# Two blocks of a language model on one core: the first memory's key projection is moved into the routing, in pieces

## The reference, cut to what matters

```python
def moe_swiglu(xn, router_w, w_gate_up, w_down):
    xf = xn.reshape(-1, d_)
    logits = (xf @ router_w).astype(jnp.float32)
    top_v, top_i = lax.top_k(logits, TOP_K)
    top_w = jax.nn.softmax(top_v, axis=-1)
    ...
    for e in range(N_EXPERTS):
        out = out + combine[:, e:e + 1] * swiglu(xf, w_gate_up[e], w_down[e])

def memory_read(q, mem_n, w_mem_kv):
    kv = mem_n @ w_mem_kv
    k, v = jnp.split(kv, 2, axis=-1)
    logits = jnp.einsum('bshd,bmhd->bhsm', q, k) * (d ** -0.5)
    ...

def hybrid_layer(x, mem, ...):
    proj = rmsnorm(x, pre_g) @ w_in
    ...
    y_mem = memory_read(mem_q, rmsnorm(mem, mem_norm_g), w_mem_kv) * jax.nn.silu(mem_g)
```

## Time and profile before

| | us |
|---|---|
| median of 3 runs (lowest, highest) | 2167.52 (2166.28, 2169.9) |
| the profiled execution, its own time | 2169.45 |
| its span in the trace | 2167.3 |
| TensorE busy | 2136.8 |
| VectorE busy | 1591.6 |
| ScalarE busy | 1332.4 |

### The profile page before, as it was taken

One profiled execution on the slowest core, in us unless ns is written; L12 is line 12 of the kernel. 1 busy time (PEld: TensorE's weight loads), 2 busy tenths in 40 slices (PEclk: granted clock), 3 DMA queues, 4 the chain that ended last, 5 costly groups with the idle time before them and its releaser, 6 DMA issues.

```text
span 2167.3 us, 27831 instructions
## 1 busy us (share of the span) xinstructions
PE 2136.8 (99%) x10935; PEld 1813.2 (84%) x10935; DVE 1591.6 (73%) x1339; ACT 1332.4 (61%) x1151; POOL 78.2 (4%) x67
## 2 busy tenths in 40 slices
PE   7999999999998999999999999999999999999998
PEld 5988888888787888888888888888888898898987
DVE  5577555466766888888888888888896667675665
ACT  4475534455656777777777777777665555456553
POOL 3100000000000000000000000000110000000000
PEclk9999999999998999999999999999999999999999
DMA  8554665555538999999999999999996534455442
GB/s 282 157 190 151 224 193 177 188 180 164 195 136 301 348 377 381 374 381 375 388 376 379 378 379 375 381 380 374 389 383 219 176 125 156 157 180 175 137 153 81
DMA packets 249166, 569.70 MB, mean 263 GB/s; under 512 B 12169, under 2 KB 14353, under 8 KB 248817
## 3 DMA queue, kind: packets, MB, share of 16 engines
q1 hardware_dynamic: 242368, 546.41, 70.5%
q0 software_dynamic: 5136, 16.70, 2.3%
q10 hardware_dynamic: 1568, 5.31, 0.6%
HBM read 562.60 MB, written 5.78 MB: 262 GB/s over the span
## 4 chain that ended last, share of the span: by engine, by line
PE 93%; DVE 3%; DMA 2%; ACT 1%; issue 0%; SPq 0%; DVEq 0%; ACTq 0%
PE bank L917 35%; PE bank L1178 9%; PE bank L1179 9%; PE bank L1182 9%; PE bank L923 9%; PE bank L1226 5%; PE bank L1219 5%; PE bank L1221 5%; PE bank L964 3%; DMA ring<-w_in 1%; DVE halves_r L2194 1%; DMA ring<-moe_w_down 1%; DVE w_low L2622 0%; PE bank L1321 0%; DMA ring<-w_out 0%; PE bank L990 0%
## 5 line engine op out<-in xcount | busy, mean ns | idle before, releaser
L2622 DVE TENSOR_TENSOR w_low<-ring,w_high 128x4096 fp32r<-128x4096 f32 x167 | 736.5, 4421 | 80.5 <-ACT w_high L1901 80.3
L1901 ACT ACTIVATE w_high<-ring 128x4096 fp32r<-128x4096 f32 x167 | 607.1, 3636 | 232.7 <-DMA ring<-moe_w_gate_up 137.9
L917 PE MATMUL bank<-halves_r,xT_high 128*128 128x512 f32 (+1 forms) x1856 | 562.3, 381 | 4.8 <-ACT halves_r L1671 3.2
L2194 DVE TENSOR_TENSOR halves_r<-ring,halves_r 128x2048 fp32r<-128x2048 f32 x175 | 391.2, 2264 | 155.1 <-ACT halves_r L1671 153.0
L917 PEld LDWEIGHTS bank<-halves_r,xT_high 128*128 128x128 f32 x1856 | 343.6, 189 | 71.7 <-issue 5.6
L1671 ACT ACTIVATE halves_r<-ring 128x2048 fp32r<-128x2048 f32 x175 | 326.4, 1892 | 111.8 <-DMA ring<-w_in 51.8
L1178 PE MATMUL bank<-w_high,xg_high 128*128 128x512 f32 x896 | 354.7, 396 | 1.7 <-DVE xg_low L2599 1.7
L1179 PE MATMUL bank<-w_high,xg_low 128*128 128x512 f32 x896 | 349.5, 390 | 0.0
L917 PE MATMUL bank<-halves_r,xT_low 128*128 128x512 f32 (+1 forms) x928 | 348.5, 380 | 0.0
L1182 PE MATMUL bank<-w_low,xg_high 128*128 128x512 f32 x896 | 221.6, 389 | 0.0
L917 PEld LDWEIGHTS bank<-halves_r,xT_low 128*128 128x128 f32 x928 | 175.3, 189 | 31.7
(11 more groups left out here) (392 smaller groups left out, 2312.8 us busy)
## 6 DMA issues: line engine op xcount, KB each, us to landing
ring<-moe_w_gate_up SPq DMA_DIRECT2D x224, 1024.0 KB, 10.6
ring<-moe_w_down SPq DMA_DIRECT2D x112, 1024.0 KB, 9.9
ring<-w_in SPq DMA_DIRECT2D x108, 1024.0 KB, 5.1
ring<-w_out SPq DMA_DIRECT2D x24, 1024.0 KB, 4.9
ring<-ffn_w_gate_up SPq DMA_DIRECT2D x22, 1024.0 KB, 5.2
ring<-ffn_w_down SPq DMA_DIRECT2D x11, 1024.0 KB, 4.9
ring<-w_mem_kv SPq DMA_DIRECT2D x8, 1024.0 KB, 5.2
ring<-w_branch_attn SPq DMA_DIRECT2D x4, 1024.0 KB, 5.1
```

The source lines that it names most:

```text
L917: return pe.matmul(o[:, a:a + n], x[:, c, b * P:(b + 1) * P], w[:, k, col:col + n], **flags)
L1901: act.activation(high_slot(k), ring[:, ring_r.slot(names[k]), :], ACT.Copy).then_inc(w_high_in[r], 1)
L2194: dve.tensor_tensor(raw_view(half, halves_r), raw_view(half), top_view(half).bitcast(F32), ALU.subtract).then_inc(raw_low_in, 1)
L2622: dve.tensor_tensor(w_low[:, slot, :], ring[:, slot, :], high_slot(k).bitcast(F32), ALU.subtract).then_inc(w_low_in[r], 1)
```

## The change

1. In the first block, `MK` of layer 0 joins the ring behind `WO`; SyncE issues its two halves ahead of the first expert's tiles, and `RAW_AT` and `TOP_AT` deal the halves otherwise. In the second block `MK` of layer 0 is gone. `MK` of layer 1 stays.
2. The 16 transposes of the memory move ahead of the transposes of block 0 of the tokens. ScalarE and VectorE form `mgk_high` and `mgk_low` (memory by gain, 8 chunks of 128x256 each) between the parts of the norm.
3. TensorE's 96 key products are cut in eight pieces (`memory_keys(k, h, top)`) and stand between the routing steps; the last 16 products stand between the gather and the first expert.
4. The three router products of a chunk become two: high by both parts of the router in one product of 16 columns, low by high in one of 8. VectorE adds the two parts.
5. The keys go over the DRAM: ScalarE copies them out of the banks behind the high part of expert 0's second tile and issues a transfer of 0.5 MB; GpSimd fetches them back in the second block.
6. VectorE makes the low part of expert 0's first tile in two halves around the parts of `xg_low`, and the weights of the routing later.
7. In the second block `MV` of layer 0 is made for both token blocks per half: high products of half 0, the scatter, low products, high products of half 1, the `P` transposes, low products.
8. TensorE's overflow body moves behind the second block. It is reached by a branch of its own and left by another; past it leads one jump at the program's end.

```diff
-RAW_AT, TOP_AT = (6, 7, 2, 3, 4), (5, 0, 1, 8)
+RAW_AT, TOP_AT = (2, 3, 4, 6, 7), (1, 5, 8, 0)
...
+    j += norm_jobs("E") if l == 1 else []
     j += norm_jobs("2", l, blocks=(0,)) + [("WO", l, 1, 1)]
...
-    "MK0 MK1 MV0 P00 P01 P10 P11 MV1 XB0 XB1 XB2 XB3 Z0 Z1 DT MQ0 MQ1 DN XT0 XT1 CB0 CB1 MG0 MG1 AC "
+    "MV0 MV1 P00 P01 P10 P11 XB0 XB1 XB2 XB3 Z0 Z1 DT MQ0 MQ1 DN XT0 XT1 CB0 CB1 MG0 MG1 AC "
...
-FIRST_HALVES = len(halves_of(first_tiles(0) + first_tiles(1)))
+FIRST_HALVES = len(halves_of(first_tiles(0) + first_tiles(1) + [("MK", 0)]))
...
                 by_block(("WO", l, 0), ("WO", l, 0), 1)
+                if l == 1:
+                    for b in range(TB):
+                        norm_turn(("E",), b, memS, (mem_x, b + 1))
                 norm_turn(("2", l), 0, xs, (norm_x, 4 * l + 3))
...
-                    pe.matmul(o[:, 8 * b:8 * b + 8], xT_high[:, c, s], router_high[:, c, :], start=first, stop=False)
-                    pe.matmul(o[:, 8 * b:8 * b + 8], xT_low[:, c, s], router_high[:, c, :], start=False, stop=False)
-                    mm = pe.matmul(o[:, 8 * b:8 * b + 8], xT_high[:, c, s], router_low[:, c, :], start=False, stop=last)
+                    pe.matmul(o[:, at_b:at_b + 2 * EXPERTS], xT_high[:, c, s], router_both[:, c, :], start=c == 0, stop=False)
+                    mm = pe.matmul(o[:, at_b:at_b + EXPERTS], xT_low[:, c, s], router_high[:, c, :], start=False,
+                                   stop=c == KC - 1)
...
+            def memory_keys(k, h, top):
+                half = (("MK", 0), h)
+                w = high_half(half) if top else low_half(half)
+                pe.wait_ge(mg_ready, 4 * h + 4)
+                if top and h == 0:
+                    keys[k] = begin(("EK", k))
+                cs = list(enumerate(half_chunks(*half)))
+                for j, a in ((2 * k, 0), (2 * k + 1, SEQ)):
+                    piece = cols(j, a)
+                    for q, c in cs:
+                        mm = piece(keys[k], mgk_high, w, c, q, start=top and h == 0 and q == 0 and a == 0,
+                                   stop=not top and h == 1 and q == len(cs) - 1 and a == SEQ)
+                        if top:
+                            mm = piece(keys[k], mgk_low, w, c, q, start=False, stop=False)
                 return mm
 
             logits = begin(("RT",))
             route_rows(logits, 0)
+            memory_keys(0, 0, True)
+            memory_keys(0, 0, False)
             norm_turn(("2", 1), 1, xs, (norm_x, 8))
+            memory_keys(1, 0, True).then_inc(top_free[tops.slot((("MK", 0), 0))], 1)
             pe.wait_ge(*drained(("X", "2", 1, 1, 1)))
             route_rows(logits, 1).then_inc(*end(("RT",)))
-            for b in range(TB):
-                norm_turn(("E",), b, memS, (mem_x, b + 1))
+            memory_keys(1, 0, False).then_inc(*raw_end((("MK", 0), 0)))
+            memory_keys(0, 1, True)
             pe.wait_ge(rt_mask, 1)
...
+            memory_keys(1, 1, True).then_inc(top_free[tops.slot((("MK", 0), 1))], 1)
+            def last_keys():
+                memory_keys(0, 1, False).then_inc(*end(("EK", 0)))
+                memory_keys(1, 1, False).then_inc(*end(("EK", 1)))
-            more = experts("m", sel_ready)
-            with pe.If(more > 0):
...
+            more = experts("m", sel_ready, last_keys)
+            pe.br_cond(more > 0, "tensor_overflow", "tensor_second_block")
...
+                if l == 0:
+                    weigh(("MV", l), [("MV0", [rows(0)]), ("MV1", [rows(1)])], l, x=mg, ready=mg_in,
+                          between={0: last_scatter, 1: norm_turns})
...
+            pe.br("tensor_done")
+            with nc.body("tensor_overflow", parent=home):
...
                 lower("2", l, 0)
...
+                    memory_low(range(KC // 2))
+                    link(dve.tensor_copy(lt_r, lt))
+                    link(dve.tensor_copy(ones_r, ones))
+                    residual_part(("WO", l, 1, 1), 1, 1)
+                    memory_low(range(KC // 2, KC))
+                    norm(1, 4 * l + 4, norm2_row)
...
                 if r == "m":
                     overflow()
-                    routing_weights()
+                    first_tile_low(0)
...
                 gathered(r, [("GX", r, 0), ("GX", r, 1)], 0)
                 if r == "m":
+                    first_tile_low(1)
+                    routing_weights()
```

More of the change, by code:

```diff
@@ L382, in kernel_program @@
             banks.lay(ffn_jobs(), kept=("FD",), silent=silent)
-    banks.lay([("RT",), *norm_jobs("2", 1, blocks=(1,)), *norm_jobs("E"), ("RK",)])
+    banks.lay([("RT",), *norm_jobs("2", 1, blocks=(1,)), ("EK", 0), ("EK", 1), ("RK",)], silent=silent)
     tiles.lay(expert_tiles("m"), EXPERTS, offsets=expert_slots())
@@ L569, in kernel_program @@
         xg_high = rounded("xg_high", [KC, P], xT_at)
+        early = Views(NHIGH * TILE)
+        mgk_high = rounded("mgk_high", [KC, SEQ], arena_at + 4 * early.at)
+        early(KC, SEQ)
+        memT_first = early(KC // 2, SEQ)
+        early = Views(NHIGH * TILE + TILE + P)
+        mgk_low = rounded("mgk_low", [KC, SEQ], arena_at + 4 * early.at)
+        early(KC, SEQ)
+        kmT_out = shaped(x_rows, 4, SEQ)
         rt = Views(ARENA - 256)(256)
@@ L946, in weigh @@
                         mm.then_inc(top_free[tops.slot(half)], 1)
-                    if between is not None and h == between[0]:
-                        between[1]()
+                    if between is not None and h in between:
+                        between[h]()
                     w = low_half(half)
@@ L1510, in _ @@
                 pe.wait_ge(*drained("YS1", l))
-                out_tile(2, between=(1, lambda: branch_turn("YR", yr, (ret_y, l + 1))))
+                out_tile(2, between={1: lambda: branch_turn("YR", yr, (ret_y, l + 1))})
                 last_out_tile()
+            pe.br("tensor_done")
+            with nc.body("tensor_overflow", parent=home):
+                pe.wait_ge(moe_done, 1)
+                for s in range(NSLOT):
+                    pe.sem_inc(f_tile_free[s], F_CREDIT)
+                for s in range(NBANK):
+                    pe.sem_inc(f_bank_free[s], F_CREDIT)
+                for n in range(2):
+                    pe.wait_ge(*drained(("Y", "m", n), EXPERTS - 1))
+                experts("f", f_sel_ready)
+                for n in range(2):
+                    pe.wait_ge(*drained(("Y", "f", n), EXPERTS - 1))
+                pe.wait_ge(f_done, 1)
+                pe.br("tensor_second_block")
+            nc.switch_bb("tensor_done", parent=home)
         @block.gpsimd
@@ L1825, in mixer @@
                     split(("FU", 0), (0,))
+                else:
+                    act.wait_ge(second_in, 16 * SECOND_LOADS)
+                    for job in norm_jobs("E"):
+                        act.wait_ge(*drained(job))
+                    for c in range(KC):
+                        src = memT_first if c < KC // 2 else memT[1]
+                        act.activation(mgk_high[:, c, :], src[:, c % 4, :], ACT.Copy,
+                                       scale=par_all[:, 0, 8 + c:9 + c]).then_inc(mem_copied, 1)
+                    split(("MK", 0), (1,))
                 norm(1, drained(("WO", l, 1, 1)))
@@ L1950, in experts @@
                     act.dma_start(hn_dram.ap().rearrange("(b p) d -> p b d", p=P), xs[:]).then_inc(hn_y_out, 16)
+                    for k in range(2):
+                        copy_out(kmT_out[:, 2 * k:2 * k + 2, :], ("EK", k), scale=HD ** -0.5)
+                    for k in range(2):
+                        act.wait_ge(*drained(("EK", k)))
+                    act.dma_start(km_dram.ap(), x_rows).then_inc(hn_y_out, 16)
+                    act.activation(memT[0], memT_first, ACT.Copy).then_inc(mem_copied, 1)
                     act.wait_ge(flag_ready, 1)
@@ L1958, in _ @@
             mixer(0)
[L1959 removed]
+            act.activation(router_high, router, ACT.Copy).then_inc(router_high_in, 1)
             ffn()
@@ L2487, in route @@
                 row8 = slots_row[:, 0:8]
[L2488 to L2495 removed]
                 dve.wait_ge(*full(("RT",)))
[L2497 removed]
+                both = out_of(("RT",))[:, 0:4 * EXPERTS].rearrange("p (b k e) -> p b k e", b=TB, k=2)
+                link(dve.tensor_copy(shaped(rt[:, 0:16], TB, 8), both[:, :, 0, :]))
+                link(dve.tensor_tensor(shaped(rt[:, 0:16], TB, 8), shaped(rt[:, 0:16], TB, 8), both[:, :, 1, :], ALU.add))
                 dve.sem_inc(*fr(("RT",)))
@@ L2678, in expert, with first_tile_low @@
                             output_low(r, e)
+                def first_tile_low(half):
+                    slot, a = tiles.slot(names[0]), half * HALF
+                    dve.wait_ge(w_high_in["m"], 1)
+                    ins = dve.tensor_tensor(w_low[:, slot, a:a + HALF], ring[:, slot, a:a + HALF],
+                                            high_slot(0)[:, a:a + HALF].bitcast(F32), ALU.subtract)
+                    if half:
```

(3 more changed lines are left out.)

148 lines of the change are left out of this document (79 added, 69 removed).

## The result

The changed kernel takes 2156.95 us (median of 4 runs, 2155.77 to 2158.86), the kernel before beside it 2167.53: ratio 0.9948, 95% interval 0.9936 to 0.9960, or 10.6 us less. The forecast was 2154.6, with a range of 2149 to 2161.5.

| stretch | before | after | difference |
|---|---|---|---|
| start to the end of `WO`'s second-last block | 652.00 | 653.03 | +1.03 |
| from there to expert 0 | 32.13 | 28.17 | -3.96 |
| expert 0 to the end of expert 7 | 952.62 | 953.86 | +1.24 |
| from there to `X0` | 30.58 | 19.52 | -11.06 |
| `X0` to the end | 499.97 | 502.52 | +2.55 |

A forecast was written before the change was run, and what follows sets the result against it. TensorE, busy 2136.8 of 2167.3 us, was taken as the bound. Routing 3.5 plus behind the experts 9.6 less experts' start 0.2 made 12.9 us: 2169.45 to 2156.5 profiled, median 1.9 below, 2154.6; range 2149 to 2161.5.

The forecast's parts named there:

- The bound: Whole kernel: TensorE, busy 2136.8 of 2167.3 us, bounds it; other engines count only where TensorE waits for them.
- The routing: `WO`'s second-last block to expert 0: products sum to 28.3 us, plus 0.3 of waits; 3.5 us gained, bounds none to 5.
- The covers: Routing: key products laid over TensorE's waits for other engines, each 0 to 1 us thicker than what it covers.
- The start of the experts: Expert 0's second tile: VectorE's low part done at 688.2, wanted at 689.7; 0.2 us lost, up to 1.5.
- Behind the experts: Expert 7 to `X0`: 19.8 us against 30.58, 10.8 gained, behind a new wait of 4.4; net 9.6, bounds 8 and 14.
- The clock at `X0`: Behind the new wait of 4.4 us at `X0`, the clock falls and costs 1.2 us (0 to 3).
- The queue: SyncE's weight transfers: the fourth expert tile lands at about 691, before 693.7 when wanted; cost nothing.
- 2 (the jump costs on): Behind expert 7: the jump isn't what costs 2.41, or the new branch costs as much; 3.9 less gained, 2158.5; chance 0.12.
- 3 (nothing from the routing): Routing: covers missed or clock stays down, expert 0 starts at 684 as before, 2158.1; chance 0.15.
- 4 (no wait at `X0`): At `X0`: new wait mostly not there and the clock holds; 4 more gained, 2150.6; chance 0.13.
- 5 (the clock falls behind 24 transposes): Routing's start at 652: clock falls behind 24 transposes in a row, costing 1.5, 2156.1; chance 0.06.
- 6 (fed late): Expert stage: weights come late and TensorE waits from the fourth tile on; 12.5 lost against 9.6 gained, 2170.4; chance 0.04.

The follow-up runs named there:

- experiment 4: Changed kernel without 80 of the 96 key products of the routing (work left out, keys wrong): 2160.08 us, ratio 0.9960 to the kernel before.
- experiment 6: Changed kernel with the router products apart again, 48 in all instead of 32: 2160.08 us, ratio 0.9963 to the kernel before.
- experiments 1 and 2: Kernel before with TensorE's overflow body moved behind the program's last product (1: 2162.61 us), or left in place but cut short (2: 2164.23 us).
- The second profile: Profile of the changed kernel run again without any edit: 2156.41 us, ratio 0.9941 to the kernel before.
- experiment 9: Changed kernel with the ring's halves dealt as before (`RAW_AT` and `TOP_AT` undone): 2174.62 us, ratio 1.0024 to the kernel before.
- experiment 8: Changed kernel with `xT`'s low parts ahead of `X0`'s low halves, and its high parts between `X0`'s high halves: 2149.62 us, ratio 0.9912.
- experiments 5 to 8: 5: changed kernel again, 2156.41 us; 7: changed kernel, last 16 key products ahead of the gather, 2157.76 us; 6 and 8 have their own lines.
- experiment 10: Experiment 8's kernel with TensorE's overflow body back between the experts and the second block: 2154.83 us, ratio 0.9932 to the kernel before.

## Why the prediction was right, step by step

**The bound.** TensorE, and stretches read by its busy share: right. The first stretch came out by the sum of its products. In the second TensorE is busy for 15.06 of 19.52 us and `X0` waits for VectorE, as the prediction had counted it.

**The routing, 3.5 forecast, 3.96 measured** (28.17 us against a sum of 28.3 and 0.3 of waits). The sum of products was right within 0.1 us, and the 0.3 of waits are not there. The covers are as thin as I had put them, 0.2 to 0.7 us. What the prediction undersold is why it pays: experiment 4 shows that the products in the holes gain by themselves, 3.3 us: without them five waits come back, and 17 us of half clock; and experiment 6 that the joined router products are part of that. The clock of the kernel before isn't a fixed loss: 32.13 in the profile that I read, 30.5 in two others. Of the 3.96, up to 1.6 was that draw. So what was forecast well is the stretch after; that the gain came out so near 3.5 is in part luck, and against the shorter 30.5 it would have been 2.3.

**The start of the experts, 0.2 forecast.** No wait there; the low part of the second tile ended 0.5 us before its use. The experts took 1.24 us more in the first profile and 0.56 in the second, within what they differ by anyhow.

**Behind the experts, 10.8 forecast ahead of the clock, 11.06 measured.** Part by part: counted from E, the end of expert 7, with the forecast in brackets: scatter at E+3.62 (3.65), VectorE's additions at E+4.28 (4.3), norm ended at E+12.5 (12.6), a wait at the transposes of 0.34 (0.6 and 0.35), `X0` at E+19.52 (19.8) behind 4.01 (4.4). The reading that the wait of 2.41 was the branch's and not VectorE's rested on the earlier trace rows; experiments 1 and 2 show that it is the skipped body's, and not VectorE's.

**The clock at `X0`, 1.2 forecast, 2.4 measured.** This is the term that was mis-sized. The price was taken from the fall of the earlier trace rows, 1.5 behind a gap of 2.41, and put lower; the wait of 4.0 brings the clock down in all seven profiles that have it, in three for 3.4 us and in four, the two of the changed kernel among them, for 6.8. Against the 500.2 from `X0` to the end without a fall it costs 1.4 or 2.4. So the two places gave 15.0 where the forecast had 14.3, and 2.5, 1.2 and 1.0 went off behind `X0`, in the experts and ahead of it all, where it had 1.2, 0.2 and nothing: 10.2 instead of 12.9. The second profile, with less of the chance, has 12.4.

**The queue, nothing.** Right under the new dealing. The fourth tile's transfer was issued at 681.4, with its weights there for ScalarE at 692.9 at the latest:

```profile
692.87 3.62 ACT L1970 ACTIVATE w_high<-ring 128x4096 fp32r<-128x4096 f32 x1
```

Its first product stood at 698.2, 1.7 behind the end of the high part. But the prediction passed over what the two tuples do; experiment 9 prices the question at 17 us.

**The rivals.** 2 (the jump costs on): refuted by 71 ns and no gap. 3 (nothing from the routing): refuted. 4 (no wait at `X0`): refuted in this kernel, and made true in experiment 8, where it gives 6.8 instead of my 4: the wait and, behind it, its clock. 5 (the clock falls behind 24 transposes): refuted, the clock stayed at 1.00 behind 653.03. By the Trainium skill, TensorE: Matmul & The Clock Gate, Part 4, a transpose doesn't count as busy in the same way; this trace shows no effect of it. What did come ahead of a fall without a gap was 24 router products in a row, in the one profile of experiment 6. 6 (fed late): refuted for this dealing; under the old one it is what happens, at expert 0 already.

Still open is how long the clock of the kernel before is down in an execution. Its nine executions beside experiments 5 to 8 suggest that this is a part of their spread: five with a mean clock of 0.996 had spans of 2164.9 to 2166.4 us, four with 0.994 or 0.995 had 2168.0 to 2169.1. Beside the other experiments the groups overlap (0.997 with 2168.2 us, 0.995 with 2165.8). The profile of experiment 10 has no fall at all and a mean clock of 1.000, as has one more of its executions (2150.7 us); the three with 0.999 took 2153.0 to 2153.6. A fall behind the gap in those three would explain why its median is further from that of experiment 8 than 2.3 us, but no trace shows it.

## What to carry to other kernels

Where a chain on other engines makes TensorE wait, fill the holes with products that are due anyway: here 96 products in the holes took less time than 16 of them, since waits and half clock came back without the others. Cut them by the length of the holes, and place them by what they cover, since the same 16 products ahead of the gather instead of behind it cost 1.9 us more. When work moves, look at what it used to cover: the keys had covered VectorE's work ahead of `X0`, and the exchange of two steps on VectorE and on ScalarE gave two thirds of the whole change once more. And ask of a buffer table which late reader holds the slot that the next stage wants first.

## What the runs showed of the hardware

- A conditional branch of TensorE over the whole overflow body took 6.1 to 6.7 us in three profiles and held products back by 2.2 to 2.8; over some 20 instructions it took 210 ns, and into the code that follows 71 ns. The table of waits put the gap down to VectorE each time.
- Behind a gap of 2.41 us the clock fell in one kernel and behind 2.80 and 2.17 in two others it didn't: products of 128x256 followed in the first, of 128x512 in the others. No run shows that this is the reason; each is one profile, and how long the clock is down also differs between executions of one kernel.
- TensorE's clock fell behind 24 products of 8 columns in a row without a gap (half rate for 3.4 us), and not behind 16 products of 16 and 8 columns in seven others. The fall is seen in one profile.
- The clock is down for 3.4 or 6.8 us, or for 13.7 or 17.1, at a place where the kernels profiled have the same products and waits: two profiles can differ by 1.6 us by that alone. It differs between executions of one kernel too. The four of the changed kernel in the result have mean clocks of 0.998 (spans 2157.1 and 2156.2 us) and 0.999 (2154.0 and 2154.2); 0.999 leaves, by an estimate from the span, at most 6.5 us at half clock in all, less than the 6.8 that the profiled one has at `X0` alone.
